# Another order in the opening of a decoder layer: when two weight units and the history rows are begun, and where two activation tiles stand among the conditioning products

## The reference

```
mod = (silu(c) @ w_ada + b_ada)            # w_ada: 1024 x 6144
shift_m, scale_m, gate_m, shift_f, scale_f, gate_f = split(mod, 6)
h = rms_norm(x, g_pre_mix) * (1 + scale_m) + shift_m
u, q, k, v, z_pool, z_att = split(h @ w_in, IN_SPLITS)      # w_in: 1024 x 7680
u_ext = concat([pool_hist, u])             # 15 rows of history for each sample
...                                        # pooling, attention, merge, FFN
```

## Time and profile before

| | us |
|---|---|
| median of 3 runs (1050.75 to 1052.26) | 1052.15 |
| the profiled execution, its own time | 1055.94 |
| its span | 1054.1 |
| PE busy in the span | 1021.0 |
| DVE, ACT, POOL busy | 480.1, 393.9, 108.9 |
| mean granted clock of PE | 0.984 |

### The profile page before, as it was taken

The page is one execution under the profiler, slowest core; times in us unless marked ns, Lnnn a source line. Parts: engine busy times, 40 slices in busy tenths (PEclk is TensorE's granted clock), DMA queues, the critical chain, the costliest instruction groups (busy, mean ns, idle before and its releaser), DMA issues.

```text
span 1054.1 us, 20546 instructions
## 1 busy us (share of the span) xinstructions
PE 1021.0 (97%) x8658; PEld 972.3 (92%) x8658; DVE 480.1 (46%) x878; ACT 393.9 (37%) x633; POOL 108.9 (10%) x157
## 2 busy tenths in 40 slices
PE   5999999999999999999899998999999999999997
PEld 3899999999999999998889986899999999999996
DVE  6733324332443243327946445655556565522323
ACT  5234423442243224432113335554544445322232
POOL 1000300040004000425603000000000000000000
PEclk8999999999999999999999998999999999999998
DMA  9966676667666876329967770466666666665422
GB/s 319 292 231 213 216 227 237 214 202 247 237 205 207 259 251 232 122 64 366 382 211 232 226 251 32 148 213 220 223 226 219 228 220 204 184 224 187 125 58 81
DMA packets 226183, 222.30 MB, mean 211 GB/s; under 512 B 6269, under 2 KB 189949, under 8 KB 225309
## 3 DMA queue, kind: packets, MB, share of 16 engines
q1 hardware_dynamic: 226009, 220.85, 63.6%
q10 hardware_dynamic: 84, 0.15, 0.0%
HBM read 213.56 MB, written 96.03 MB: 294 GB/s over the span
## 4 chain that ended last, share of the span: by engine, by line
PE 89%; DVE 3%; SPq 2%; DMA 2%; ACT 1%; issue 1%; DVEq 0%; ACTq 0%
PE acc L1458 74%; PE psS L1652 2%; PE psT L1666 2%; DMA ada_first<-in_w_ada 1%; SPq L383 1%; PE psS L1855 1%; DMA raw<-in_w_proj_pool 1%; PE psS L1640 1%; PE acc L1551 1%; PE psT L1680 1%; DVE w_lo L967 1%; PE psT L1700 1%; PE psS L1638 1%; PE acc L1746 1%; PE psT L1541 1%
## 5 line engine op out<-in xcount | busy, mean ns | idle before, releaser
L1458 PE MATMUL acc<-act_hi,w_hi 128*128 128x260 f32 x1856 | 380.2, 286 | 4.6 <-DVE mixS L1320 1.9
L1458 PE MATMUL acc<-act_hi,w_lo 128*128 128x260 f32 x1856 | 374.0, 283 | 0.0
L1458 PE MATMUL acc<-act_lo,w_hi 128*128 128x260 f32 x1856 | 373.7, 283 | 0.0
L967 DVE TENSOR_TENSOR w_lo<-raw,w_hi 128x1024 fp32r<-128x1024 f32 (+1 forms) x148 | 190.4, 1287 | 354.3 <-ACT w_hi L699 351.9
L1458 PEld LDWEIGHTS acc<-act_hi,w_hi 128*128 128x128 f32 x1856 | 286.1, 189 | 10.0 <-DVE w_lo L967 5.2
L1458 PEld LDWEIGHTS acc<-act_hi,w_lo 128*128 128x128 f32 x1856 | 286.3, 189 | 0.0
L1458 PEld LDWEIGHTS acc<-act_lo,w_hi 128*128 128x128 f32 x1856 | 286.3, 189 | 0.0
L699 ACT ACTIVATE w_hi<-raw 128x1024 fp32r<-128x1024 f32 (+1 forms) x148 | 154.8, 1046 | 181.6 <-PE acc L1458 172.5
L1458 PE MATMUL acc<-g_hi,w_hi 128*128 128x260 f32 x352 | 71.6, 285 | 0.0
L1458 PE MATMUL acc<-g_hi,w_lo 128*128 128x260 f32 x352 | 70.8, 282 | 0.0
L1458 PE MATMUL acc<-g_lo,w_hi 128*128 128x260 f32 x352 | 70.6, 282 | 0.0
(11 more groups left out here) (282 smaller groups left out, 1014.2 us busy)
## 6 DMA issues: line engine op xcount, KB each, us to landing
out_k_sample<-in_cache_k_w SPq DMA_DIRECT2D x89, 368.0 KB
out_v_sample<-in_cache_v_w SPq DMA_DIRECT2D x89, 368.0 KB
raw<-in_w_in SPq DMA_DIRECT2D x60, 512.0 KB, 6.3
raw<-in_w_up SPq DMA_DIRECT2D x44, 512.0 KB, 5.5
ada_last<-in_w_ada SPq DMA_DIRECT2D x12, 1024.0 KB, 9.4
ada_first<-in_w_ada SPq DMA_DIRECT2D x9, 1024.0 KB, 9.1
raw<-in_w_down SPq DMA_DIRECT2D x16, 512.0 KB, 4.7
out_k_sample<-in_cache_k_w SPq DMA_DIRECT2D x16, 511.0 KB
```

The source lines that it names most:

```text
L967: dve.tensor_tensor(w_lo[PLACE[n]][:, 0:cols], raw[:, n % RAW, 0:cols], w_hi[PLACE[n]][:, 0:cols].bitcast(F32), ALU.subtract).then_inc(lo_ ...
L1458: ins_ = pe.matmul(acc[b][:, half, 0:HALF], w, x[:, t, half * HALF:(half + 1) * HALF], start=first and i == 0 and j == 0, stop=last and i ...
```

## The change

SP: behind the eighth ada unit it now waits until the seventh (`ada_in[6]`) has landed, before it begins units 2 and 3; the history rows come behind unit 3 instead of ahead of unit 2. PE and DVE: the transposes and sums of the history rows stand behind unit 3 of pair 0 instead of ahead of unit 2. PE: both activation tiles of a couple stand together, behind the even ada unit of the next couple, and the odd ada unit and the folds come behind them. DVE: `ada_evac` of the next couple stands behind `normed` instead of between the two tiles.

```diff
             for s in range(2, SADA):
                 ada_load(s)
-            sp.dma_start(hist_rows[...], ins["state_pool"][0]...).then_inc(hist_loaded, 16)
+
+            sp.wait_ge(ada_in[SADA - 2], 16)
...
             for n in range(2, PAIRS * NU):
                 pair_unit(n)
+                if n == 3:
+                    sp.dma_start(hist_rows[...], ins["state_pool"][0]...).then_inc(hist_loaded, 16)
                 beside(n)
...
                 modulated(2 * j + 1)
-                if j < 3:
-                    ada_evac(2 * j + 2)
-                    ada_evac(2 * j + 3)
                 lo_of(xT[:, 2 * j + 1, :], 2 * j + 1, 0)
                 if j < 3:
                     normed(2 * j + 2)
                     normed(2 * j + 3)
+                    ada_evac(2 * j + 2)
+                    ada_evac(2 * j + 3)
             split(2)
-            dve.wait_ge(hist_turned, 1)
-            for gi in range(4):
-                ...
+            def sum_hist():
+                dve.wait_ge(hist_turned, 1)
+                for gi in range(4):
+                    ...
...
                             split(SPLITS[N[s] + 2])
+                        if p == 0 and k == 3:
+                            sum_hist()
...
             fold(0)
             fold(1)
-            ada(2)
-            ada(3)
...
-            for j in range(1, 4):
-                first_units(2 * j - 2)
-                fold(2 * j)
-                fold(2 * j + 1)
-                first_units(2 * j - 1)
+            for j in range(4):
                 if j < 3:
                     ada(2 * j + 2)
+                first_units(2 * j)
+                first_units(2 * j + 1)
+                if j < 3:
                     ada(2 * j + 3)
-            first_units(6)
-            first_units(7)
-            pe.wait_ge(hist_loaded, 16)
-            (8 transposes of hist_rows)
+                    fold(2 * j + 2)
+                    fold(2 * j + 3)
+
+            def turn_hist():
+                pe.wait_ge(hist_loaded, 16)
+                (8 transposes of hist_rows)
...
                             blocks(s, slot, ...).then_inc(unit_done, 1)
+                        if p == 0 and k == 3:
+                            turn_hist()
```

More of the change, by code:

```diff
@@ L439, in _ @@
                 ada_load(s)
-            sp.dma_start(hist_rows[0:NB * POOL_HIST, :], ins["state_pool"][0].rearrange("b t n -> (b t) n")).then_inc(hist_loaded, 16)
+            sp.wait_ge(ada_in[SADA - 2], 16)
             def cached(i, kv):
@@ L494, in _ @@
                 pair_unit(n)
+                if n == 3:
+                    sp.dma_start(hist_rows[0:NB * POOL_HIST, :], ins["state_pool"][0].rearrange("b t n -> (b t) n")).then_inc(hist_loaded, 16)
                 beside(n)
@@ L1095, in _ @@
                     normed(2 * j + 3)
+                    ada_evac(2 * j + 2)
+                    ada_evac(2 * j + 3)
             split(2)
-            dve.wait_ge(hist_turned, 1)
-            for gi in range(4):
[L1099 to L1103, removed]
+            def sum_hist():
+                dve.wait_ge(hist_turned, 1)
+                for gi in range(4):
+                    win = 2 ** (gi + 1)
+                    at = gi // 2 * 512 + gi % 2 * 240
+                    src = psT[:, at:at + 240].rearrange("p (k b t) -> p k b t", k=2, b=NB)[:, :, :, 16 - win:]
+                    ins_ = dve.tensor_reduce(hist_sum[:, 2 * gi:2 * gi + 2, :], src, AX_X, ALU.add)
+                ins_.then_inc(hist_ready, 1)
             def step(p, j):
@@ L1601, in first_units @@
                 half_split([("pair", 0, k) for k in range(2)], [ready(("pair", 0, k)) for k in range(2)], t, t == 0, t == KT - 1, 0, t // 2 + 1)
-            for j in range(1, 4):
-                first_units(2 * j - 2)
-                fold(2 * j)
-                fold(2 * j + 1)
-                first_units(2 * j - 1)
+            for j in range(4):
                 if j < 3:
                     ada(2 * j + 2)
+                first_units(2 * j)
+                first_units(2 * j + 1)
+                if j < 3:
                     ada(2 * j + 3)
-            first_units(6)
-            first_units(7)
-            pe.wait_ge(hist_loaded, 16)
[L1614 to L1618, removed]
+                    fold(2 * j + 2)
+                    fold(2 * j + 3)
+            def turn_hist():
+                pe.wait_ge(hist_loaded, 16)
+                for k in range(KT):
+                    at = (k % 4) * NB * POOL_HIST + 512 * (k // 4)
+                    ins_ = pe.transpose(psT[:, at:at + NB * POOL_HIST], hist_rows[0:NB * POOL_HIST, k * P:(k + 1) * P],
+                                        ident[0:NB * POOL_HIST, 0:NB * POOL_HIST])
+                ins_.then_inc(hist_turned, 1)
             def step(p, j):
```

## The result

| | before | changed |
|---|---|---|
| first comparison, median of 5 runs, us | 1052.26 (1050.75 to 1057.27) | 1060.4 (1057.0 to 1063.23) |
| ratio, 95% interval | | 1.0071 (1.0045 to 1.0097) |
| second comparison, on one chip, medians of 35 and 12 runs, us | 1052.22 (1050.13 to 1057.73) | 1058.11 (1056.88 to 1064.05) |
| ratio, 95% interval | | 1.0063 (1.0045 to 1.0082) |
| profiled execution of the first, span, us | 1054.1 | 1060.2 |

The changed kernel is slower by 0.6 to 0.7%: 8.1 us between the first medians, 5.9 between the second. Slower was forecast, but by 4.27 us, to 1056.4 with a range from 1053.4 to 1058.8: 1060.4 lies outside it, the 1058.11 of the second comparison inside.

What follows compares the result with a forecast made beforehand. The prediction took PE's progress through its instruction list to bound the kernel. Its terms, 1.58 + 2.24 - 0.30 + 0.75 = +4.27 us, added to the 1052.15 us median, gave 1056.4 us, range 1053.4 to 1058.8.

Steps and rivals of the forecast that it cites:

- What bounds the opening: In the opening, PE's own way through its list sets the time, not the last ada unit's landing at 39.83.
- Folds of couple 1: On PE these folds start at 31.76 us instead of 30.18, +1.58 us.
- Period of a couple: From folds to folds on PE: 7.24 us instead of 5.83 and 6.41, +2.24 us over two periods.
- From the last folds to unit 2: On PE, unit 2 waits for DVE's split and starts 5.97 us behind these folds instead of 6.27, -0.30 us.
- the clock would fall again: Rival: new PE idle times bring half clock back, costing 1.7 us, to 1058.1; chance 0.12 together with unit 2 late.
- History transposes: On PE they come later in the list, behind unit 3, and add 0.75 us.
- Transfers: Opening DMAs: the last ada unit lands earlier, worth nothing; no loss taken for unit 2, 2.2 us if its bound held.
- The clock earlier at tiles 0 and 1: Rival: PE at full clock from 26.54, 1.50 us less, +2.8 in sum, to 1054.9; chance 0.18.

Runs made afterwards that it cites:

- e2: Kernel before with only the changed order of tiles, ada units, folds and DVE copies; transfers and history rows as before; 1058.37 us, ratio 1.0048.
- e6: Changed kernel with the second tile of each couple behind the folds and DVE's copies between the tiles as before; 1054.84 us, ratio 1.0024.
- e9: Changed kernel with tile 5 alone moved behind the last folds and DVE's copies for couple 3 as before; 1055.83 us, ratio 1.0032.
- e7: Changed kernel with history rows ahead of unit 2, tile 1 behind ada unit 3, and from couple 2 tiles, folds and copies as before; 1050.9 us, ratio 0.9978.
- e8: e7 with 20 more matmuls on PE, products nobody reads, behind the first folds; 1050.82 us, ratio 0.9985.
- e10: e7 with transfers as before the change: history rows ahead of unit 2, no wait for ada unit 6; 1051.92 us, ratio 0.9991.
- e1: Kernel before with only the changed transfers and the history rows moved behind unit 3; tiles, folds and copies as before; 1052.75 us, ratio 1.0001.
- e4: Changed kernel with 12 more matmuls on PE, products nobody reads, in the idle time behind the last folds; 1057.35 us, ratio 1.0044.
- e5: The changed kernel run again with no edit, against the kernel before; 1058.11 us, ratio 1.0063.
- e3: Changed kernel with the history rows turned and summed ahead of unit 2 again; 1057.08 us, ratio 1.004.

## Why the prediction was off, step by step

**What bounds the opening: right.** PE's list, not the last ada unit. In the changed kernel that unit was issued at 26.51 and landed 11.0 us later, at 37.5, 2.3 us earlier than before, and PE took it at 44.76.

```profile
ada_first<-in_w_ada SPq DMA_DIRECT2D x1, 1024.0 KB, 11.0
```

**Folds of couple 1: +1.58 forecast, +1.52 measured, in part by luck** (31.70 against 30.18). Tile 0 began at 25.28, not 24.94, since ada unit 2 was 0.6 us later in this execution, and it took 2.77 us, not 2.59; against that the clock was full at about 29.1 us, not 29.95, so tile 1 took 2.03 us, not 2.51. Both together end 0.04 us from the forecast. The wait for DVE's copy was 0.55 us, not about 0.7.

**Period of a couple: 7.24 forecast, 7.33 and 7.35 measured.** Together with the folds of couple 1 that is +3.96 at the last folds against +3.82. e2 shows that it is this order; in e6, with a tile behind the folds again, the wait for `act_hi` is gone from couples 1 and 2 and the period is 6.8, the wait of 0.55 us for DVE's copy staying. e6 and e9 put DVE's copies back as well, and no run parts the two.

**From the last folds to unit 2: -0.30 forecast, +1.59 measured. This is the step that failed, and twice.** The first error is a wait that the prediction did not look for. It took the 6.27 us before as DVE's split plus the history transposes; but unit 2 waits also for ACT's copy of unit 0 out of its accumulator. Before the change the transposes lay beside that copy and hid it. The distance without a fall of the clock was 6.23 to 6.32 us with the transposes (before, e7, e8, e10) and without them (e1, e4): 0.3 us of the error. The second error is of weight, not of mechanism: that the clock would fall again stood among the rivals, at 1.7 us, with a chance of 0.12 for it and a late unit 2 together. It did fall in all four profiles of kernels with the 1.6 us of idle time behind the last folds (changed, e5, e2, e3), and in none of those where that time was filled or covered (e4, e6, e9). It costs 1.5 us, the other part of the 1.89 us between forecast and measurement.

The low price also rests on a wrong reading. The prediction says that the clock had fallen once, at 23.12, behind 2.2 us of idle time. In the opening alone it had fallen twice. The trace of the kernel before has another stretch at half clock, from 16.30, behind idle times of 0.55 and 1.52 us, less than the 1.76 us that the prediction itself put behind the last folds:

```profile
14.03 1.07 PE L1510 MATMUL psS<-ada_first,siluT 128*32 128x256 f32 x16 [0.55 <-DMA ada_first<-in_w_ada]
16.62 1.93 PE L1510 MATMUL psS<-ada_first,siluT 128*32 128x256 f32 x16 [1.52 <-DMA ada_first<-in_w_ada]
```

```profile
16.30:19.70 3.40, 3.08 (x23) 1.81 (x23) 0.71 (x2) 1.11 (x2) 0.00 (x0) 0.50 1.09 352
```

Such an idle time can bring the fall and need not: this one, of 1.4 to 1.5 us ahead of ada unit 1, stands in all twelve profiles, in code that the kernels share, and the clock fell behind it in four (before, e7, e8, e10). Behind the 1.6 us it fell four times of four; that it always does is not shown.

The Trainium skill, "TensorE: Matmul & The Clock Gate", section "HAM oscillation — how this bites in real kernels", warns of waits between groups of matmuls. Here the trace agrees in kind, with 1.54 us between e4 and the changed kernel; the waits of the page's example are longer than the 1.61 us that were enough here.

**History transposes: +0.75 forecast, +0.83 measured**, right in kind; with the copy by ACT known it would have been seen that before they had been free.

**Transfers: nothing forecast, nothing measured** (e1, together with the history rows: 1.0001). No engine waited for unit 2, which was issued at 34.63.

**The clock earlier at tiles 0 and 1: not as the rival had it.** Tile 0 ran at half clock as before, and the clock was full in the course of tile 1, at about 29.1 us and not at 26.54. In e10, where PE ran the same two steps at the start (ada unit 2, tile 0), it was full at 26.6.

With both errors mended the forecast would have been 1.58 + 2.24 + 1.54 + 0.75 = 6.1 us; the measured terms are 1.52 + 2.44 + 1.59 + 0.83 = 6.4 us, and 5.9 was measured in the second comparison. The 8.1 us of the first are 1.7 us above these terms, and where they come from stays open. What is on record is the clock of these five runs: its mean was 0.982 to 0.986 in all five runs of the changed kernel, and never the 0.988 that e5 has in three of its twelve. Whether the change itself makes such executions more frequent is neither shown nor excluded.

## What to carry to other kernels

Between an instruction and the one that needs its result over two other engines, count what the waiting engine still has to do; here one tile of 1.5 us put back behind the last folds (e9) brought unit 4 2.8 us forward, with the fall of the clock gone as well. A block that seems to cost its own time can lie beside a wait that shows only when the block is gone, so look for every semaphore of the next instruction, the freeing of its accumulator too. And a new idle time on PE like the 1.6 us here has two prices, its own and the half clock that may follow it: look through the whole trace for every stretch at half clock and the idle time ahead of it, and give the second price a weight by how often it came. Last, the opening's profile and the median of the runs can disagree, as in e7, e8 and e10; compare executions of like mean clock before an order is called better.

## What the runs showed of the hardware

Behind an idle time of 1.61 us after two folds came 3.4 us of half clock in four of four profiles, and with 24 records of products that nobody reads in its place (e4) it did not come. Behind an idle time of 1.4 to 1.5 us ahead of ada unit 1 it came in four of twelve. The time of one kernel ranges over 7 us from execution to execution, and the mean granted clock roughly goes with it: in e5 1057 us at 0.988, 1064 at 0.982.
